# Scaling one item earlier in a scan, weight units in pieces, clears split in two, output in four stores

## What is computed

```python
y = y.reshape(bb, ll, SSD_D_INNER) * jax.nn.silu(z)
y = rms_norm(y.reshape(bb, ll, SSD_N_GROUPS, SSD_D_INNER // SSD_N_GROUPS), ...)
return y.reshape(bb, ll, SSD_D_INNER) @ w_out
```

## Time and profile before

| | us |
|---|---|
| median of 3 runs | 1740.91 (1739.31 to 1741.22) |
| the profiled execution, its own time | 1741.44 |
| its span | 1739.6 |

### The profile page before, as it was taken

The page is one execution under the profiler, slowest core; times in us unless marked ns, Lnnn a source line. Parts: engine busy times, 40 slices in busy tenths (PEclk is TensorE's granted clock), DMA queues, the critical chain, the costliest instruction groups (busy, mean ns, idle before and its releaser), DMA issues.

```text
span 1739.6 us, 21615 instructions
## 1 busy us (share of the span) xinstructions
PE 1549.9 (89%) x8520; PEld 791.7 (46%) x8520; DVE 609.6 (35%) x1282; ACT 372.6 (21%) x763; POOL 256.8 (15%) x250
## 2 busy tenths in 40 slices
PE   5999999999899899999787887899899988888786
PEld 3434445454444455555343443445455544444443
DVE  2533447767732314321111112657512211111112
ACT  2311148898510100000000000237100000000000
POOL 2000003544310011011010012110001010101001
PEclk9999999999999899999999999999999999999999
DMA  9687658998350699999999999931679999999996
GB/s 372 238 317 290 260 200 237 325 316 295 128 191 13 240 384 424 426 425 426 427 427 427 428 425 398 350 124 42 227 298 425 425 426 425 426 426 427 426 426 256
DMA packets 141920, 572.74 MB, mean 329 GB/s; under 512 B 22360, under 2 KB 79208, under 8 KB 111120
## 3 DMA queue, kind: packets, MB, share of 16 engines
q1 hardware_dynamic: 121296, 525.49, 75.5%
q0 software_dynamic: 14784, 26.11, 4.2%
q10 hardware_dynamic: 5760, 20.06, 3.4%
HBM read 543.52 MB, written 49.25 MB: 341 GB/s over the span
## 4 chain that ended last, share of the span: by engine, by line
PE 52%; DMA 35%; DVE 5%; ACT 4%; issue 3%; SPq 0%; ACTq 0%; POOL 0%; DVEq 0%; POOLq 0%
DMA mem<-in_moe_w_down_dram 18%; DMA mem<-in_moe_w_gate_dram 14%; PE bank L1974 13%; PE bank L626 9%; PE bank L1987 7%; PE bank L997 6%; PE bank L2397 3%; ACT mem L1051 2%; PE bank L361 2%; PE bank L942 2%; DMA consts<-in_consts_dram 2%; PE bank L2497 2%; PE bank L2444 1%; PE bank L1968 1%; PE bank L2424 1%
## 5 line engine op out<-in xcount | busy, mean ns | idle before, releaser
L1974 PE MATMUL bank<-mem 128*64 128x256 f32 x4160 | 502.9, 393 | 68.5 <-DMA mem<-in_moe_w_gate_dram 43.0
L1974 PEld LDWEIGHTS bank<-mem 128*64 128x64 f32 x4160 | 293.9, 136 | 276.0 <-issue 46.2
L1987 PE MATMUL bank<-mem 128*64 128x512 f32 x1040 | 241.9, 608 | 47.0 <-DMA mem<-in_moe_w_down_dram 43.1
L1920 POOL DMA_INDIRECT ys_dram<-mem x61 | 61.3, 1005 | 766.8 <-DVE mem L2219 697.6
L626 PE MATMUL bank<-mem 128*128 128x512 f32 x384 | 171.2, 598 | 0.9 <-DMA mem<-in_ssd_w_in_dram 0.9
L2146 ACT ACTIVATE mem<-bank 128x256 f32<-128x256 f32 x65 | 25.0, 384 | 676.6 <-PE bank L1974 659.3
L1987 PEld LDWEIGHTS bank<-mem 128*64 128x64 f32 x1040 | 71.4, 139 | 178.1 <-issue 117.9
L2219 DVE TENSOR_TENSOR mem<-bank,mem 128x512 f32<-128x512 f32 x65 | 45.0, 692 | 235.1 <-PE bank L1987 179.0
L2198 DVE TENSOR_TENSOR mem<-mem,bank 128x256 f32<-128x256 f32 x65 | 27.4, 421 | 269.4 <-PE bank L1974 159.2
L942 PE MATMUL bank<-mem 128*128 128x512 f32 x256 | 117.4, 602 | 0.0
L626 PEld LDWEIGHTS bank<-mem 128*128 128x128 f32 x384 | 70.8, 190 | 97.6 <-issue 94.9
(11 more groups left out here) (338 smaller groups left out, 1508.4 us busy)
## 6 DMA issues: line engine op xcount, KB each, us to landing
mem<-in_moe_w_up_dram SPq DMA_DIRECT2D x64, 2048.0 KB, 8.6
mem<-in_moe_w_down_dram SPq DMA_DIRECT2D x64, 2048.0 KB, 13.7
mem<-in_moe_w_gate_dram SPq DMA_DIRECT2D x63, 2048.0 KB
mem<-in_mod_w_dram SPq DMA_DIRECT2D x24, 2048.0 KB
ys_dram<-consts SPq DMA_DIRECT2D x55, 512.0 KB, 8.2
mem<-in_ssd_w_in_dram SPq DMA_DIRECT2D x10, 2048.0 KB
mem<-ac_dram ACTq DMA_DIRECT2D x32, 512.0 KB, 5.6
mem<-in_ssd_w_out_dram SPq DMA_DIRECT2D x4, 2048.0 KB
```

Of the source, the lines that this page charges most:

```text
L1920: pool.indirect_dma_start(ys_dram[l].rearrange("r (c n) -> (r c) n", c=2), bass.IndirectOffsetOnAxis(r_toi[:, j:j + 1], 0), yb[:, j % 2, : ...
L1974: mm = nc.tensor.matmul(bank[half * BR:(half + 1) * BR, 0:HF], lhsT=x[:, k], rhs=w[k][:, half::2], start=(k == 0), stop=(k == KD - 1), ski ...
L1987: mm = nc.tensor.matmul(bank[half * BR:(half + 1) * BR, :], lhsT=ht[:, k // 2, k % 2 * BR:(k % 2 + 1) * BR], rhs=w[:, k, half * COLS:(half ...
```

## The change

1. `norm` of the group before moves from item 2 of a group to item 1, directly behind `mean`.
2. The clears are split: layer 1's 23 stay in the scan; layer 0's 32 are issued in `moe_sp` behind units 6 and 13 and ahead of unit 0.
3. The three units of the last expert of each layer are loaded in two DMAs each, with a semaphore of its own for the first piece (4 of 8 chunks for gate and up, 3 of 4 for down). TensorE waits for the first piece at chunk 0 and for the rest at chunk 4 or 3.
4. `stream_rows_dve` for tiles 0 and 1 stands ahead of the late add of tile 3.
5. The output is stored in four parts of 256 KB (two halves of the columns for each tile), the left ones by SP, the right ones by ScalarE's queue, each as soon as its add is done.
6. Three semaphores are merged into others: `at_in` into `sc_in` (waits for 80 instead of 32), `at_g1` into `fin_in`, `rt_wA` into `rt_shift`.

```diff
...
@@ -1177,7 +1177,6 @@
                     mean(g - 1)
-                if g and k == 2:
                     norm(g - 1)
...
@@ -1433,7 +1431,7 @@
             if half == 0:
-                pe.wait_ge(rt_wA, l + 1)
+                pe.wait_ge(rt_shift, 2 * l + 1)
                 pe.wait_ge(rt_m, t0 + t)
...
@@ -1815,14 +1814,12 @@
-        def clear_ys_sp(sp):
+        def clear_ys_sp(sp, l):
             zero = bc(consts[:, C_ZERO:C_ZERO + P], 1, KD)
-            sp.wait_ge(sc_mix, 4)
-            for l in range(2):
-                for m in range(YS[l] // P):
-                    sp.dma_start(ys_dram[l][m * P:(m + 1) * P, :].rearrange("p (k n) -> p k n", k=KD),
-                                 zero).then_inc(ys_zero, 16)
+            for m in range(YS[l] // P):
+                sp.dma_start(ys_dram[l][m * P:(m + 1) * P, :].rearrange("p (k n) -> p k n", k=KD),
+                             zero).then_inc(ys_zero, 16)
@@ -1841,6 +1838,8 @@
                     load_unit(sp, n0 + n)
+                    if n == 13:
+                        clear_ys_sp(sp, 0)
             else:
@@ -1876,11 +1875,18 @@
                         ring_in[slot_of(at + u)], 16)
-            for n in range(at + 3 * BODIES * LOOP, last):
+            for n in range(at + 3 * BODIES * LOOP, last - 3):
                 if l:
...
                     load_placed(n)
+            for n in range(last - 3, last):
+                which = moe_unit(n - n0)[0]
+                source = unit_source(n) if l else expert_source(l, which, placed(slice(E - 1, E)))
+                sp.wait_ge(*used(last_of[n]))
+                to, cut = unit(n, k=(KD, KD, KF)[which]), TAIL[which]
+                sp.dma_start(to[:, 0:cut, :], source[:, 0:cut, :]).then_inc(tail_in[which], 16)
+                sp.dma_start(to[:, cut:, :], source[:, cut:, :]).then_inc(ring_in[slot_of(n)], 16)
@@ -1968,8 +1974,16 @@
-            def gate_or_up(bank, x, w):
+            def tail_wait(which, k, n):
+                if k == 0:
+                    pe.wait_ge(tail_in[which], 16 * (l + 1))
+                if k == TAIL[which]:
+                    ring(n, None)
+
+            def gate_or_up(bank, x, w, tail=None):
                 for k in range(KD):
+                    if tail is not None:
+                        tail_wait(tail[0], k, tail[1])
                     for half in range(2):
@@ -1981,8 +1995,10 @@
-            def down(bank, ht, w):
+            def down(bank, ht, w, tail=None):
                 for k in range(KF):
+                    if tail is not None:
+                        tail_wait(2, k, tail)
                     for half in range(2):
@@ -2007,17 +2023,19 @@
                     pe.wait_ge(moe_h, at_round(i, BODIES, MB[l] + b - 1))
-                ring(n, i)
-                gate_or_up(psum[2 * (b % 2)], xgT[:, q % 2, :, b % 2 * BR:(b % 2 + 1) * BR],
-                           chunks(n)).then_inc(moe_gate, 1)
+                if b < NB[l] - 1:
+                    ring(n, i)
+                gate_or_up(psum[2 * (b % 2)], xgT[:, q % 2, :, b % 2 * BR:(b % 2 + 1) * BR], chunks(n),
+                           (0, n) if b == NB[l] - 1 else None).then_inc(moe_gate, 1)
...
                     pe.wait_ge(rt_ov, l + 1)
-                ring(n, i)
-                gate_or_up(psum[2 * (b % 2) + 1], xgT[:, q % 2, :, b % 2 * BR:(b % 2 + 1) * BR],
-                           chunks(n)).then_inc(moe_up, 1)
+                if b < NB[l] - 1:
+                    ring(n, i)
+                gate_or_up(psum[2 * (b % 2) + 1], xgT[:, q % 2, :, b % 2 * BR:(b % 2 + 1) * BR], chunks(n),
+                           (1, n) if b == NB[l] - 1 else None).then_inc(moe_up, 1)
@@ -2027,11 +2045,12 @@
                 n = n0 + UNIT_AT[2, place_of(l, j)]
-                ring(n, i)
+                if j < NB[l] - 1:
+                    ring(n, i)
                 pe.wait_ge(moe_hc, at_round(i, BODIES, MB[l] + j + 1))
...
                     pe.wait_ge(moe_ya, at_round(i, BODIES, MB[l] + j))
-                down(psum[4], hT[:, j % 2], unit(n, k=KF)).then_inc(moe_down, 1)
+                down(psum[4], hT[:, j % 2], unit(n, k=KF), n if j == NB[l] - 1 else None).then_inc(moe_down, 1)
@@ -2311,6 +2330,10 @@
                 ins = nc.vector.tensor_tensor(x, x, psum[late_bank(l, t) + half][:, :], ALU.add)
+                if l:
+                    ins.then_inc(cb_x, 1)
+            if l:
+                return
             if t < 2:
...
@@ -2384,7 +2405,7 @@
             pool.wait_ge(cb_x, NT)
-            pool.dma_start(gate1a, mod_dram[1, 0:1, 2 * D:3 * D].to_broadcast([P, D])).then_inc(at_g1, 16)
+            pool.dma_start(gate1a, mod_dram[1, 0:1, 2 * D:3 * D].to_broadcast([P, D])).then_inc(fin_in, 16)
             for n, cols in enumerate([*Q_COLS[0:2], *K_COLS, *Q_COLS[2:4]]):
@@ -2595,7 +2616,7 @@
             cos, sin = rope[:, 0], rope[:, 1]
-            dve.wait_ge(at_in, 48)
+            dve.wait_ge(sc_in, 80)
             for to, gain in ((qtab, qgain), (ktab, kgain)):
@@ -2674,8 +2695,8 @@
             stream_mean_dve(dve, 0)
+            stream_rows_dve(dve, 0)
             late_add_dve(dve, 0, 3)
-            stream_rows_dve(dve, 0)
             stream_evac_dve(dve, 0)
...
@@ -2716,6 +2737,13 @@
         out_st = sem("out_st")
+
+        def store_out(eng, half):
+            cs = slice(half * COLS, (half + 1) * COLS)
+            for t in range(NTL):
+                eng.wait_ge(cb_x, NT + 2 * t + half + 1)
+                eng.dma_start(out[0, t * P:(t + 1) * P, cs], xin[:, t, cs]).then_inc(out_st, 16)
+
         block = ctx.enter_context(nc.Block())
@@ -2749,17 +2777,16 @@
                     norm2_cols_sp(sp)
-                    clear_ys_sp(sp)
+                    sp.wait_ge(sc_mix, 4)
+                    clear_ys_sp(sp, 1)
             moe_sp(sp, 0)
...
             moe_sp(sp, 1)
-            for t in range(NTL):
-                sp.wait_ge(cb_x, NT + t + 1)
-                sp.dma_start(out[0, t * P:(t + 1) * P, :], xin[:, t, :]).then_inc(out_st, 16)
-            sp.wait_ge(out_st, 16 * NTL)
+            store_out(sp, 0)
+            sp.wait_ge(out_st, 16 * 2 * NTL)
...
```

15 lines of the change are left out of this document (7 added, 8 removed).

## The result

The changed kernel runs in 1732.75 us (median of 6 runs, 1731.69 to 1735.54), beside 1742.26 for the kernel before on the same chip in the same session (6 runs, 1739.31 to 1744.07). Ratio 0.9949, 95% interval 0.9937 to 0.9961: 0.5% faster. The prediction was 1727, with a range of 1722 to 1735. Direction and range hold. The profiled execution took 1732.35 us with a span of 1730.5, so 9.1 us less than before, where 14.0 were forecast. Two thirds of the forecast came. What is missing has two main causes: VectorE and POOL block each other in the scan, and the weight pieces land later than the whole units did. A faster clock in one place, which the forecast had left at nothing, hides part of the loss.

A forecast was written before the change was run, and what follows sets the result against it. The weight stream bounds the expert stages; TensorE, VectorE and ScalarE handing work over bound scan and output projection. 7.1 + 2.9 + 1.25 + 1.0 + 1.25 + 0.5 = 14.0 us off 1741.44 gave 1727, range 1722 to 1735.

The forecast's parts named there:

- Term: 3 x 2.4 = 7.1 us.: Scan's three group borders: scalings moved one item earlier into VectorE's idle gap save 2.4 us each, 7.1 us.
- if the gap failed at the first border, 0.3 us would go: First scan border: bound on the loss if the scalings did not fit the gap ahead of L1118, 0.3 us.
- With 2.4 us less waiting I expect full clock at all three: 2.9 us.: TensorE at the scan's borders: shorter waits remove the low clock seen at the first border; 2.9 us, ends 0 and 2.9.
- Part 2: Splitting the clears: 0 us by itself, keeps part 1 from being cut by 0 to 4 us; POOL's delay stays hidden.
- (d): Second norm's loads: ten clears to each of POOL's packets, 7.8 us of stall, 1735; chance 0.06.
- (e): Second norm's loads: engines serve clears first, POOL's loads end at 551, TensorE stalls 41 us, 1768; chance 0.05.
- (f): Second norm's loads: seventeen clears to each of POOL's packets, 18 us late, 15 of stall, 1742, no change; chance 0.02.
- part 1: Scan: scalings one item earlier, directly behind POOL's power, 7.1 us over three borders.
- Part 3: Last expert's units in pieces: first pieces let the last down start and end earlier, 1.25 us in each layer.
- 0 if both pieces land together: Last down of layer 0: lower bound on the 1.25 us gain from loading units in pieces.
- Rival (b): Last expert's units: pieces don't help because the slowest engine ends both at once; 2.5 us less, 1729.5; chance 0.08.
- Parts 4 and 5: Rows ahead of the late add save 1.0 us (0 to 1.3); output in four stores saves 0.5 (0 to 0.6).

The follow-up runs named there:

- the second profile: Changed kernel with the four scalings back at item 2, against the kernel before: 1738.98 us, ratio 0.9995.
- the third profile with waits of 1.86 us: Whole-unit version of the changed kernel with two scalings at the new place and two at the old: 1732.53 us, ratio 0.9955 to the kernel before.

## Why the prediction was right, and where it was too high

**Bound and mechanism.** Right: the scan's borders gave most of it, a microsecond there reached the end (8.25 us earlier at the first gate of layer 0, 9.1 at the end), and without the scalings' move nothing measurable is left.

**"Term: 3 x 2.4 = 7.1 us."** 5.7. The place, the order and the gap were right, the duration wasn't: "Four scalings of 2.45 us in all end at 325.45" took a duration from a place with another neighbour. The trace of before held the warning twice. There the four take 0.47, 0.47, 1.26 and 0.47 us, and the slow one starts while POOL's L895 runs. And behind the last group, where POOL only issues DMAs, the same four take 1.67:

```profile
473.51 1.67 DVE L1170 TENSOR_SCALAR mem<-mem,smalls 128x512 f32<-128x512 f32 x4 [1.15 <-POOL smalls L916]
```

At the new place POOL starts two L895 and an L902 at the same moment, because its power is what both wait for. So 4.04 us, about 1.2 past the decay at the first border and 0.2 at the others: 2.45 - 1.2 = 1.25 and twice 2.45 - 0.2 = 2.25, which are the 1.26, 2.2 and 2.2 measured. The bound "if the gap failed at the first border, 0.3 us would go" was too narrow.

**"With 2.4 us less waiting I expect full clock at all three: 2.9 us."** Right in the changed kernel's profile, and partly luck: in three other profiles with the scalings at the new place the clock fell all the same, one item ahead of the first border, and it cost 0.4 us at most. At the old place the drop is there again in the second profile, at another border and smaller, and in the third profile with waits of 1.86 us it is at none.

**Part 2.** Right: 0 us, the loads 1.6 us late for 2.1 worked out from the shares of 67.3 and 27.3%, clears issued by 554. Rivals (d), (e) and (f) fall. That part 1 needs the split was right as well: without it TensorE waits 1.68 us, and the clock behind the wait makes it 3.3.

**Part 3, "The first half is there in each case when TensorE gets free, and the second (half of 3.84 us of matmuls later) too".** This step failed, in both layers: for up's second half (waits of 1.63 and 1.36 us) and for down's first piece (1.90 and 1.88 us where none was forecast), not for the first halves of gate and up (gate's second half was 0.35 us late in layer 0). In their place the runs showed that a unit in pieces gets less of the engines beside POOL's gathers, 68% where a whole one has 74 to 75%, and that up and down land later for it. The sum of +2.5 became -1.4 and -0.5. The bound "0 if both pieces land together" left no room for a unit that lands later because it is in pieces; I took the landing from a stream at 425 GB/s, while in these last 20 us the engines are shared with the gathers. Rival (b) had the term at nothing but not its sign. The 1.7 us of this down's clock, left at 0, came and hid the loss. That was luck: in five other profiles, with pieces and without, the down of layer 0 took 5.0 to 5.35 us all the same, so it is no property of the change.

**Parts 4 and 5.** 1.0 and 0.5, as forecast, both shown by undoing them.

**The rest.** 0.3 us at the start of the scan and 0.4 between the layers have no cause that a run tells; other profiles of one and the same code differ by as much there.

So 14.0 - 1.4 (scalings beside POOL) - 0.3 - 2.65 (pieces, layer 0) + 1.7 (clock of its down) - 1.8 (pieces, layer 1) - 0.4 = 9.15, beside 9.1 between the spans. The total lay inside the range, though one term had the wrong sign in both layers.

## What to carry to other kernels

Before an instruction moves into a gap, look at what the other engines do in that gap and not only how long it is: a duration belongs to its neighbours. Splitting a transfer to start on its first part paid here only where nothing else used the DMA engines; look at which queues are active in the last stretch, and ask what the transfers behind the split one will lose. Compare shares of the engines only in stretches that begin at the same event. Where a wait remains, a start gained ahead of it is no gain, and the clock behind it can make it a loss.

## What the runs showed of the hardware

- VectorE's `tensor_scalar` on 128x512 f32 takes 0.47 to 0.49 us (four in 1.68, since their rows overlap) with POOL not computing and 1.26 to 1.28 when a POOL `tensor_tensor` runs as it starts; POOL's instruction goes from 1.03 to 1.22. The block is by whole instructions.
- A 2 MB unit cut in two by the chunks of its rows lands later than uncut when indirect gathers share the engines: the last of three such units is complete 2.2 us later in layer 1 (19.1 for 16.9 us), its first three quarters 0.5 us later, and the last down starts 0.5 to 1.4 us later. Without gathers the last one is complete 0.2 to 0.4 us later, and the last down starts 0.9 to 1.1 us earlier.
- The low granted clock followed waits of 1.24 us (down of layer 0 before, 5.35 us for 3.65), 1.68 (L942, 5.24 for 3.60) and 2.0 (up, 5.44 and 5.45 for 3.85), and in three profiles 0.81 (L942, 4.58 to 4.70), but not every wait of that length. In the two runs of the same kernel with whole units, the down of layer 0 took 3.65 us behind 1.34 us and 5.35 behind 1.32; behind 1.90 us the changed kernel's took 3.65. The runs give no rule by length.
- Holding four of layer 0's eight gathers until the last unit had landed moved the last down by 0.1 us (whole units) and 0.25 us (pieces), holding all eight by 1.4 and 3.8 us: the first four still used the engines while the last units were under way.
